# Four sequence mixers of a Trainium2 kernel: output projections taken inner chunk by inner chunk, with new step orders

## What is computed

```
# hgrn2 (8 heads of 128): projections q, f, i, og; chunked recurrence with decays exp(b)
o = rmsnorm(o, g_norm) * silu(og);                 y = o @ w_out
# mlstm (4 heads, values of 256): q, k, v, og, and gates x @ w_if of 4 + 4 columns
o = rmsnorm(h, norm_g) * sigmoid(og);              y = o @ w_out
# swa (16 heads of 64, 4 kv heads, window 128): q, k normed per head
s = q k^T / 8 - slope_h * distance, masked;        p = softmax(s with one sink per head)
y = (p @ v) @ w_o
x = x + y
```

## Time and profile before

| | us |
|---|---|
| median of 3 runs | 3394.75 (3394.45 to 3395.14) |
| the profiled execution | 3397.95, its span 3396.2 |
| PE busy | 3229.3 (95%) |
| DVE busy | 2467.2 (73%) |
| ACT busy | 1767.3 (52%) |
| mean granted clock of TensorE | 0.969 |

### The profile page before, as it was taken

The page is one execution under the profiler, slowest core; times in us unless marked ns, Lnnn a source line. Parts: engine busy times, 40 slices in busy tenths (PEclk is TensorE's granted clock), DMA queues, the critical chain, the costliest instruction groups (busy, mean ns, idle before and its releaser), DMA issues.

```text
span 3396.2 us, 64490 instructions
## 1 busy us (share of the span) xinstructions
PE 3229.3 (95%) x27210; PEld 3125.5 (92%) x27210; DVE 2467.2 (73%) x3728; ACT 1767.3 (52%) x2677; POOL 3.0 (0%) x6
## 2 busy tenths in 40 slices
PE   6899999999999999979999997999999999997899
PEld 6789899988989999879999977999988999997899
DVE  8887699887767766786676656667666667678666
ACT  4456444556544545665454535445456455457544
POOL 0000000000000000000000000000000000000000
PEclk8799999989999999989999998999999999998999
DMA  8455488434546455425555533555543555552453
GB/s 306 139 174 192 156 309 310 154 129 147 181 143 225 166 193 188 154 87 185 189 184 188 184 128 119 187 183 190 187 161 112 190 186 186 187 181 94 151 188 131
DMA packets 164351, 597.93 MB, mean 176 GB/s; under 512 B 18240, under 2 KB 18272, under 8 KB 163936
## 3 DMA queue, kind: packets, MB, share of 16 engines
q1 hardware_dynamic: 164064, 593.81, 51.9%
HBM read 592.69 MB, written 1.05 MB: 175 GB/s over the span
## 4 chain that ended last, share of the span: by engine, by line
PE 83%; DVE 12%; ACT 3%; issue 1%; DMA 1%; SPq 0%; DVEq 0%; ACTq 0%
PE ps L473 26%; PE ps L474 26%; PE ps L475 26%; DVE wlo L433 3%; DVE fa L1537 1%; ACT whi L421 1%; PE ps L1129 1%; DVE land L548 1%; DVE h L1771 0%; PE ps L1245 0%; DMA land<-w_ada 0%; DMA land<-w_in 0%; DVE fa L2348 0%; PE ps L2177 0%; PE ps L2200 0%
## 5 line engine op out<-in xcount | busy, mean ns | idle before, releaser
L473 PE MATMUL ps<-h,whi 128*128 128x256 f32 x5472 | 1546.4, 283 | 42.9 <-DVE h L747 21.2
L474 PE MATMUL ps<-h,whi 128*128 128x256 f32 x5472 | 1536.9, 281 | 0.0
L475 PE MATMUL ps<-h,wlo 128*128 128x256 f32 x5472 | 1536.1, 281 | 0.0
L433 DVE TENSOR_TENSOR wlo<-land,whi 128x1024 fp32r<-128x1024 f32 (+1 forms) x1032 | 1217.1, 1216 | 228.3 <-ACT whi L421 227.4
L421 ACT ACTIVATE whi<-land 128x1024 fp32r<-128x1024 f32 (+1 forms) x1032 | 1028.8, 1044 | 183.9 <-PE ps L475 166.4
L473 PEld LDWEIGHTS ps<-h,whi 128*128 128x128 f32 x5472 | 1037.8, 190 | 51.7 <-issue 31.5
L474 PEld LDWEIGHTS ps<-h,whi 128*128 128x128 f32 x5472 | 1037.5, 190 | 0.7
L475 PEld LDWEIGHTS ps<-h,wlo 128*128 128x128 f32 x5472 | 1037.2, 190 | 0.0
L474 PE MATMUL ps<-y,whi 128*128 128x256 f32 x1472 | 410.9, 279 | 0.0
L473 PE MATMUL ps<-y,whi 128*128 128x256 f32 x1472 | 410.9, 279 | 0.0
L475 PE MATMUL ps<-y,wlo 128*128 128x256 f32 x1472 | 410.9, 279 | 0.0
(11 more groups left out here) (425 smaller groups left out, 2892.9 us busy)
## 6 DMA issues: line engine op xcount, KB each, us to landing
land<-w_gu SPq DMA_DIRECT2D x352, 512.0 KB, 3.5
land<-w_dn SPq DMA_DIRECT2D x176, 512.0 KB, 3.7
land<-w_in SPq DMA_DIRECT2D x136, 512.0 KB, 3.8
land<-w_ada SPq DMA_DIRECT2D x96, 512.0 KB, 3.9
land<-w_up SPq DMA_DIRECT2D x88, 512.0 KB, 4.1
land<-hg_in SPq DMA_DIRECT2D x64, 512.0 KB, 4.2
land<-w_down SPq DMA_DIRECT2D x44, 512.0 KB, 4.4
land<-ple_gate SPq DMA_DIRECT2D x32, 512.0 KB, 4.0
```

Of the source, the lines that this page charges most:

```text
L433: dve.tensor_tensor(w.lo, g.slot(n), w.hi.bitcast(F32), ALU.subtract).then_inc(*D_("w_lo", n))
L473: pe.matmul(out, w.hi, x.hi, start=first, stop=False, skip_group_check=skip)
L474: pe.matmul(out, w.hi, x.lo, start=False, stop=False, skip_group_check=skip)
L475: return pe.matmul(out, w.lo, x.hi, start=False, stop=last, skip_group_check=skip)
```

## The change

1. The weights of the three output projections are laid out in another order of blocks (`OUT_BLOCKS`). Six steps `early:0` to `early:5` each take one inner chunk for six of the eight outputs (18 matmuls), and wait only for the heads of that chunk; `end` takes chunks 6 and 7 for the six outputs, then all chunks for the last two (28 blocks, 84 matmuls). Four banks are open at once. The four updates of x follow tile 4, the sum of outputs 2 and 3, tile 5 and tile 7, and the next stage's norm is written between them on ACT and DVE.
2. The step orders of all three kinds of mixer are new; `finish` and `tail` are split in `finish`, `low` and `tail`, and hgrn's `f_out` waits for the event `hq`.
3. mlstm: the gate rows are 48 fp32r matmuls in place of 32 fp32 ones (each of which is two records in the trace); ACT and DVE split the small gate weights at the stage's start.
4. swa goes by pairs of heads, 8 steps in place of 16. Four more matmuls per pair add minus the distance with the mask to the scores on PE; the slope becomes the scale of the exponential, which reads PSUM itself; DVE takes the maxima from PSUM and scales the probabilities before they are transposed; the product with the values comes out as channels by tokens and goes straight to the projection's operand. `proj:2` stands after `scores:1`, `turn_in:1` right after `turn_in:0` and `factor:1`.
5. Token mixing: in `da_scores` the q k matmuls of both maps come first, then the mask matmuls of both.

```diff
                 for tb, end in ((0, 128), (1, 384)):
                     pe.matmul(g.ps[b][:, tb * 128:end], q[p0:p1, a + tb * 128:a + tb * 128 + 128],
-                              k[p0:p1, a:a + tb * 128 + 128], start=True, stop=True)
+                              k[p0:p1, a:a + tb * 128 + 128], start=tb == 0, stop=False, skip_group_check=True)
+            for m in range(2 if kind == "a" else 1):
+                b = 3 + m if kind == "a" else 3 + i % 2
+                for end in (128, 384):
                     mm = pe.matmul(g.ps[b][:, end - 128:end], g.causal[:, 0:128], g.causal[:, 128:256], start=False,
-                                   stop=True, skip_group_check=True)
+                                   stop=end == 384, skip_group_check=True)
                 mm.then_inc(*D_("scores", st, kind, i, m))
         elif step in ("da_turn", "mla_turn"):
...
+    if before[:2] == "mx":
+        name, n0 = OUT_NAMES[before]
+        take_vector(g, dve, name, n0 + 5)
+        update_vector(g, dve, before, 0)
+        update_vector(g, dve, before, 1)
+        for k in halves(0):
+            rest_vector(g, dve, st, which, k)
+        take_vector(g, dve, name, n0 + 6)
+        update_vector(g, dve, before, 2)
+        for k in (2, 3):
+            rest_vector(g, dve, st, which, k)
+        take_vector(g, dve, name, n0 + 7)
+        for k in (4, 5):
...
-def out_bank(j):
-    return j % 3
-def out_tensor(g, pe, st, name, n0, z, per):
-    for j in range(4):
-        proj_tensor(g, pe, name, n0 + j, out_bank(j), ("x", AFTER[st], j), z,
-                    [("hz", st, k // per) for k in range(8)] if j == 0 else None)
-def out_scalar(g, act, name, n0):
-    for j in range(4):
-        take_scalar(g, act, name, *halves(n0 + j))
+EARLY = 6
+def out_blocks():
+    blocks = [(k, m) for k in range(EARLY) for m in range(6)]
+    blocks += [(k, m) for m in range(6) for k in range(EARLY, 8)]
+    return blocks + [(k, m) for m in (6, 7) for k in range(8)]
+OUT_BLOCKS = out_blocks()
+LATE = 6 * EARLY
+OUT_BANKS = {"mx0": (0, 1, 2, 3), "mx1": (0, 1, 2, 3), "mx2": (2, 6, 0, 1), "mx3": (0, 1, 2, 3)}
+def out_span(step, i):
+    return (6 * i, 6 * i + 6) if step == "early" else (LATE, 64)
+def out_tensor(g, pe, st, z, span, ready):
+    D_, W = g.m.done, g.m.when
+    name, n0 = OUT_NAMES[st]
+    for b in range(*span):
+        k, m = OUT_BLOCKS[b]
+        if b % 8 == 0:
+            g.out_tile = take_tensor(g, pe, name, n0 + b // 8)
+        if k == 0 and m % 2 == 0:
+            pe.wait_ge(*W(*g.banks.use(OUT_BANKS[st][m // 2], "x", AFTER[st], m // 2)))
+        if m == 0:
+            pe.wait_ge(*W(*ready[k]))
+        mm = mm3(pe, g.ps[OUT_BANKS[st][m // 2]][:, m % 2 * T:m % 2 * T + T], g.weights(g.out_tile)[:, b % 8 * 128:b % 8 * 128 + 128],
+                 z.chunk(k), k == 0 and m % 2 == 0, k == 7, skip=True)
+        if b % 8 == 7:
+            mm.then_inc(*D_("tile", g.out_tile))
+        elif k == 7 and m == 3:
+            mm.then_inc(*D_("out_sum", st))
+def out_ready(g, st, q):
+    name, n0 = OUT_NAMES[st]
+    return ("out_sum", st) if q == 1 else ("tile", g.index[name, n0 + (4, None, 5, 7)[q]])
...
-    prepare:1.0 v_out:1.0 gate:0.0 gate:0.1 values:0.0 cross64:1.0 sum:0.0 sum:0.1 factor:0.0 cross128:1.0 level:1.0
-    level:1.1 level:1.2 gate_out:0.0 gate_out:0.1 level:1.3 finish:0.0 level:1.4 gate:0.2 level:1.5 level:1.6
...
+    level:0.4 v_out:0.0 f:1.1 cross128:0.0 level:0.5 v:1.0 f_out:1.1 level:0.6 v:1.1 diagonal:0.0 prepare:1.0
+    v_out:1.0 gate:0.0 values:0.0 cross64:1.0 sum:0.0 sum:0.1 cross128:1.0 level:1.0 level:1.1 level:1.2 gate:0.1
+    factor:0.0 gate_out:0.0 level:1.3 gate_out:0.1 finish:0.0 level:1.4 low:0.0 gate:0.2 level:1.5 level:1.6 gate:0.3
+    diagonal:1.0 gate_out:0.2 values:1.0 finish:0.1 gate_out:0.3 early:0.0 low:0.1 sum:1.2 early:0.1 sum:1.3 early:0.2
...
-    tail:3 end:0
...
+    scores:2 finish:0 gate:1 values:2 gate_out:1 finish:1 scores:3 gate:2 gate:3 values:3 low:0 tail:2 gate_out:2
+    low:1 tail:3 gate_out:3 finish:2 finish:3 low:2 low:3 early:0 early:1 early:2 early:3 early:4 early:5 end:0
...
-            c0 = PARAM_COLS["w_if"]
+            w = gate_weights(g)
+            pe.wait_ge(*W("w_if", st))
             pe.wait_ge(*W(*g.banks.use(MISC, "if_read", st)))
             for c in range(2):
                 out = g.ps[MISC][0:4, c * T:(c + 1) * T]
                 for k in range(8):
-                    w = g.par[:, c0 + k * 8 + c * 4:c0 + k * 8 + c * 4 + 4]
-                    h = g.h.chunk(k)
-                    pe.matmul(out, w, h.hi.bitcast(F32), start=k == 0, stop=False)
-                    mm = pe.matmul(out, w, h.lo.bitcast(F32), start=False, stop=k == 7)
+                    mm = mm3(pe, out, w[:, k * 8 + c * 4:k * 8 + c * 4 + 4], g.h.chunk(k), k + c == 0, k == 7, skip=True)
             mm.then_inc(*D_("if_sum", st))
         elif step == "columns":
             token_factor_tensor(g, pe, st)
...
-    norm:0 proj:0 columns:0 factor:0 proj:1 factor:1 turn_in:0 proj:2 turn_in:1 exp:0 scores:0 scores:1 exp:1
...
+    norm:0 proj:0 columns:0 factor:0 proj:1 turn_in:0 factor:1 turn_in:1 exp:0 scores:0 exp:1 scale:0 scores:1 proj:2
...
-            c, p0, kv = i // 2, 64 * (i % 2), i // 4
-            ps = g.ps[3 + i % 2]
-            if i % 4 == 0:
-                pe.wait_ge(*W("turned_in", st, 0, i // 8))
-                pe.wait_ge(*W("turned_in", st, 1 + i // 8, i % 8 // 4))
-            pe.wait_ge(*W(*g.banks.use(3 + i % 2, "masked", st, "s", i)))
-            pe.matmul(ps[:, 0:128], M.qT[p0:p0 + 64, c * T:c * T + 128], M.kT[p0:p0 + 64, kv * T:kv * T + 128], start=True,
-                      stop=True)
-            pe.matmul(ps[:, 128:384], M.qT[p0:p0 + 64, c * T + 128:(c + 1) * T], M.kT[p0:p0 + 64, kv * T:(kv + 1) * T],
-                      start=True, stop=True).then_inc(*D_("scores", st, "s", i))
+            kv, banks = i // 2, SWA_SCORES[i % 2]
+            if i % 2 == 0:
+                pe.wait_ge(*W("turned_in", st, 0, i // 4))
+                pe.wait_ge(*W("turned_in", st, 1 + i // 4, i % 4 // 2))
+            for b in banks:
+                pe.wait_ge(*W(*g.banks.use(b, "exp", st, i)))
+            for h in range(2):
+                ps, q, k = g.ps[banks[h]], M.qT[64 * h:64 * h + 64, :], M.kT[64 * h:64 * h + 64, kv * T:(kv + 1) * T]
+                pe.matmul(ps[:, 0:128], q[:, i * T:i * T + 128], k[:, 0:128], start=True, stop=False, skip_group_check=True)
+                pe.matmul(ps[:, 128:384], q[:, i * T + 128:(i + 1) * T], k, start=False, stop=False, skip_group_check=True)
+            pe.wait_ge(*W("dist", st))
+            for h in range(2):
+                ps = g.ps[banks[h]]
+                pe.matmul(ps[:, 0:128], M.minus, M.dist[:, 0:128], start=False, stop=False, skip_group_check=True)
+                mm = pe.matmul(ps[:, 128:384], M.minus, M.dist[:, 128:384], start=False, stop=True, skip_group_check=True)
+            mm.then_inc(*D_("scores", st, i))
         elif step == "turn":
...
+            for h in range(2):
+                ps, scale = g.ps[SWA_SCORES[i % 2][h]], SWA_SLOPE[2 * i + h]
+                act.activation(S[:, h, 0:128], ps[:, 0:128], ACT.Exp, bias=nm[:, 0, h:h + 1], scale=scale,
+                               accum_out=sm[:, 0, h:h + 1])
+                e = act.activation(S[:, h, 128:384], ps[:, 128:384], ACT.Exp, bias=nm[:, 1, h:h + 1], scale=scale,
+                                   accum_out=sm[:, 1, h:h + 1])
...
+            for h in range(2):
+                dve.tensor_scalar(S[:, h, 0:128], S[:, h, 0:128], rc[:, 0, h:h + 1], None, ALU.mult)
+                last = dve.tensor_scalar(S[:, h, 128:384], S[:, h, 128:384], rc[:, 1, h:h + 1], None, ALU.mult)
+            last.then_inc(*D_("probs", st, "s", i))
```

312 lines of the change are left out of this document (190 added, 122 removed).

## The result

The changed kernel takes 3340.25 us, the median of 4 runs (3338.67 to 3341.82), against 3394.94 for the kernel before in the same measurements (4 runs, 3394.45 to 3398.47). The ratio is 0.9834, 95% interval 0.9821 to 0.9847: 54.7 us faster, where 65 were forecast. The profiled execution is the one with 3341.82 us, its span 3340.0, against 3396.2.

A forecast was written before the change was run, and what follows sets the result against it. PE was taken as the bound (busy 95%), with 78 us idle in the mixers plus clock loss. Token mixing -4, hgrn -32, mlstm -25 and swa -4 sum to -65: median 3330 us, range 3300 to 3366.

The forecast's parts named there:

- Token mixing: First block's two layers: fewer changes between 64 and 128 rows save 4 us (0 to 14), counting each layer's last step.
- hgrn, levels: Both hgrn mixers' levels: projections moved between levels save 3 us in the first half and 5 in the second, each mixer.
- 5.6 is more than any of these gaps, so they are covered: hgrn levels: one moved projection of 5.6 us outlasts PE's waits of 1.69, 2.33 and 3.04 us there.
- Rival 1: Only half the gain comes, about -30 us (3365): splits and head chains share DVE and ACT, waits return; 20%.
- hgrn, tail: hgrn's output projection: early chunks run beside sums and factors, saving 7.2 us per mixer (3 to 10).
- mlstm: mlstm mixer: faster gate rows, no wait before `values:3` and a shorter tail save 25 us (10 to 32).
- new small gaps: mlstm: steps pulled forward open small new waits, costing 2 us.
- swa: swa mixer: work by head pairs, paced by DVE, saves 4 us (from 8 slower to 15 faster).
- stage 95 to 96 long: Sign for swa: the stage lasts 95 to 96 us, with a new wait near 4 us at the first queries.
- Rival 3: Output matmuls cycling three banks keep PE at half clock, losing 89 us: 24 us slower, 3419; 8%.
- Rival 2: swa is slower: hand-overs make a pair 5 us, +9 us for the stage, total -52 (3343); 18%.
- Rival 4: Early steps find their heads no earlier; only gate rows and the mlstm gap pay, -15 us (3380); 6%.

## Why the prediction was right, and where it wasn't

The forecast of 3330 in 3300 to 3366 held, with 84% of the gain it named. Its sum did better than its parts: hgrn gave half of its 32 us, and 6.6 us more than forecast from token mixing and mlstm made up for some of it, which was luck. Of its signs the ones for hgrn failed (PE idle 19.0 and 24.4 us, where under 12 was said), and those for mlstm and for swa's first queries came. By its steps:

- **Token mixing**, -4: measured -6.8 by place. The price of a change of rows was right (six at 0.30 are 1.8, measured 2.0 for the fourth step). The step "I count only the last step of each layer" was undersized: the third counts with 1.4. Of the first two the saving did turn into a wait for ACT, so -14 was too much as a sum. The Trainium skill's "TensorEngine Tiling (Array Packing)", Key Properties, says that changing the tiling mode drains TensorE; the 2.0 us for six changes fewer agree.
- **hgrn, levels**, -8 in each with 1.4 given back: this failed. Measured -2.2 and +2.5. The step was "5.6 is more than any of these gaps, so they are covered". The two gaps that a projection went into (levels 0.4 and 1.3) were covered. The 3.04 at level 1.4 is two steps behind the moved gate, and was 3.52 in the changed kernel. And the forecast counted 1.4 us for the places that the projections leave, and nothing for their splits on DVE: the second mixer had 2.5 and 2.6 us more before `cross64` and `values:0`, which went when DVE's splits were light. DVE was busy 133 of 172 us in the mixer, and 119 of 140 in the level part of the changed kernel; that should have been read as a second bound. Rival 1 had this mechanism, and its sum (only half comes) was closer for hgrn.
- **hgrn, tail**, -7.2 and -0.77: measured -7.5 with the start of the next stage. The sum was right. Head pair 3 was there as forecast, 19.5 and 19.0 us after the values (20 was said), but it didn't set the end alone. PE waited 2.71 for pair 2, until 14.8 and 14.2, and ran its 120 last matmuls without another wait, 0.131 us each for the half clock at their beginning; it came to the last 84 at 20.6 and 20.0, a us behind pair 3 (its row is below). The later wait for L1771, 1.4, became 0.6.
- **mlstm**, -25: measured -28.3. Rows -8.5 (forecast -8.3), the wait before `values:3` -6.65 (all of it), the tail 43.4 to 30.3 (forecast 31.4). The "new small gaps" of +2 didn't come.
- **swa**, -4: measured -2.6, and -4.4 with the next stage's start. The wait of 4.45 at the queries was forecast as 4.5. The half clock behind it wasn't in the sum (7.4 us of matmuls there, 3.7 lost), but the length of the attention was right: pair 6 was scaled 42.7 us after the first scores, forecast 41.5 to 44.5, with the last pairs 2.9 to 4.3 us apart. The -2.6 is one execution, and the same code took 97.6 to 101.1 us elsewhere, so the term is known to some 2 us. The sign "stage 95 to 96 long" doesn't follow from the forecast's own places, which give 98 to 100.
- **Rival 3** (banks and clock) is out: the early matmuls start 0.117 us apart, 0.131 as the mean of 120 behind a wait, and mlstm's stage has clock 1.00 with the same cycling. The case of the Trainium skill's "TensorE: Matmul & The Clock Gate", section "A second HAM failure mode: psum-queue depth-cycling", where banks cycled in each iteration let the clock oscillate, doesn't appear here.
- **Rival 2** is out for this order. With `proj:2` moved back it would nearly have come true: 109.3 us, 7.0 more than before, where it said 9.
- **Rival 4** is out: the tails of hgrn gave 7.5 us each.

DVE's row for head pair 3 of the second hgrn mixer, changed kernel; the values had ended at 3091.41:

```profile
3109.70 0.69 DVE L1449 TENSOR_TENSOR ra<-fa,ra 128x512 fp32r<-128x512 f32 x1 [0.70 <-ACT ra L2405]
```

## What to carry to other kernels

When work is moved into a gap, price three things: the gap it fills, the gap it opens where it stood, and what it brings along on the other engines. Where two engines both have much work in a stretch (here 119 us each in 140), its new order was worth little, and the gain was at its end: a product whose last inputs come late was taken by inner chunk, so that only the late chunks wait. In swa a long projection was worth more between the first short steps, which wait for other engines, than ahead of them: 99.7 us against 109.3.

## What was not expected of the hardware

A wait of the same length was followed by matmuls at full clock in one execution and at half clock in another. The same program place in two kernels with the same code there, the values of the first half in the second hgrn mixer; first the changed kernel, then the one with grouped early steps:

```profile
3049.40 0.67 PE L2274 MATMUL ps<-fa 128*128 128x256 f32 x2 [2.60 <-DVE fa L2540]
```

```profile
3050.51 0.92 PE L2268 MATMUL ps<-fa 128*128 128x256 f32 x2 [2.62 <-DVE fa L2534]
```

Both waited 2.6 us, after a projection at 0.117 us a matmul. The next sum began 5.19 us later in the first and 6.85 in the second. Of the seven kernels with this order two had 5.2 us there and five 6.8 to 6.9. What decides it no run shows. Such a place is worth 1.7 us and a mixer has several; I take that for the main reason why the same code spreads by 2 to 3 us a stage. A single execution can't settle a difference of 2 us. The idle times help where they repeat: the wait before `cross64` was 3.87 to 3.89 in all seven. That has to be seen first, for the wait at level 1.4 of the same seven ran from 0.92 to 3.52.
